# Seven block products in place of eight for the down product of both feed-forward blocks, and another order of the state space products

## What is computed

```
h = h + 0.5 * (silu(n @ w_gate) * (n @ w_up)) @ w_down     # n = RMSNorm(h), d_ff = 2816; first block
z = RMSNorm(h) @ w_in                                       # latents, u, gates
attn = attention of the latents; ssm = GLU(GELU(S5 forward(u) + S5 backward(u) + D * u))
h = h + (sig(g_a) * attn @ W_oa + sig(g_s) * ssm @ W_os) @ W_out
h = h + 0.5 * SwiGLU(RMSNorm(h))                            # second block
out = RMSNorm(h)
```

## Time and profile before

| | us |
|---|---|
| median of three runs | 2460.91 (2458.86 to 2461.21) |
| the profiled execution, its own time | 2459.75 |
| its span in the trace | 2457.8 |
| TensorE busy | 2233.3 |
| VectorE busy | 1286.4 |
| ScalarE busy | 863.3 |
| GpSimd busy | 580.9 |
| mean granted clock of TensorE, share of 2.4 GHz | 0.955 |

### The profile page before, as it was taken

How to read it: one execution, slowest core, us unless ns; L and a number is a source line. 1 busy time by engine, 2 the same in 40 slices (tenths; PEclk the granted TensorE clock), 3 DMA queues, 4 the chain that set the end, 5 groups by cost and what they waited for, 6 DMA issues and landing times. The chain is left out here.

```text
span 2457.8 us, 27322 instructions
## 1 busy us (share of the span) xinstructions
PE 2233.3 (91%) x10338; PEld 1853.9 (75%) x10338; DVE 1286.4 (52%) x1944; ACT 863.3 (35%) x1396; POOL 580.9 (24%) x500
## 2 busy tenths in 40 slices
PE   4999999989996969998958998799599999999997
PEld 3878888868885968887847776577488888878886
DVE  7675555533335226972347777451755555543444
ACT  5423232322223214143127776321432323322232
POOL 5347777600000011220002221000433233310000
PEclk8999999999997989998979999899699999999999
DMA  2323232272112363322420000241222222255111
GB/s 103 101 95 104 90 104 93 100 300 89 49 31 95 116 98 129 103 77 59 130 80 5 6 6 1 98 172 39 95 98 90 69 86 71 101 199 190 48 52 69
DMA packets 169729, 223.63 MB, mean 91 GB/s; under 512 B 32064, under 2 KB 121664, under 8 KB 169088
## 3 DMA queue, kind: packets, MB, share of 16 engines
q1 hardware_dynamic: 169600, 221.90, 27.9%
HBM read 162.58 MB, written 59.28 MB: 90 GB/s over the span
## 5 line engine op out<-in xcount | busy, mean ns | idle before, releaser
L48 PE MATMUL psum<-f_B_hi,f_A_hi 128*128 128x512 f32 x1232 | 483.7, 393 | 1.4 <-ACT rows L879 1.1
L50 PE MATMUL psum<-f_B_hi,f_A_lo 128*128 128x512 f32 x1232 | 479.8, 389 | 0.0
L49 PE MATMUL psum<-f_B_lo,f_A_hi 128*128 128x512 f32 x1232 | 479.7, 389 | 0.0
L48 PE MATMUL psum<-f_wd_hi,f_hh 128*128 128x512 f32 x704 | 275.7, 392 | 13.2 <-DVE f_hh L1030 13.2
L49 PE MATMUL psum<-f_wd_lo,f_hh 128*128 128x512 f32 x704 | 275.6, 391 | 0.0
L50 PE MATMUL psum<-f_wd_hi,f_hh 128*128 128x512 f32 x704 | 275.4, 391 | 0.0
L48 PEld LDWEIGHTS psum<-f_B_hi,f_A_hi 128*128 128x128 f32 x1232 | 231.4, 188 | 49.9 <-issue 2.5
L50 PEld LDWEIGHTS psum<-f_B_hi,f_A_lo 128*128 128x128 f32 x1232 | 231.4, 188 | 48.5
L49 PEld LDWEIGHTS psum<-f_B_lo,f_A_hi 128*128 128x128 f32 x1232 | 231.5, 188 | 47.2
L1028 DVE TENSOR_TENSOR f_wd_lo<-f_wd_raw,f_wd_hi 128x1024 fp32r<-128x1024 f32 x88 | 107.8, 1225 | 300.3 <-ACT f_wd_hi L916 300.3
L916 ACT CAST f_wd_hi<-f_wd_raw 128x1024 fp32r<-128x1024 f32 x88 | 92.8, 1054 | 360.0 <-PE psum L50 343.9
(11 more groups left out here) (306 smaller groups left out, 4079.1 us busy)
## 6 DMA issues: line engine op xcount, KB each, us to landing
f_raw<-ffn_w_gate SPq DMA_DIRECT2D x22, 1024.0 KB, 5.4
f_raw<-ffn_w_up SPq DMA_DIRECT2D x22, 1024.0 KB, 5.4
hidden<-rows SPq DMA_DIRECT2D x22, 1024.0 KB, 6.3
f_h_raw<-hidden SPq DMA_DIRECT2D x88, 256.0 KB, 2.7
f_wd_raw<-ffn_w_down SPq DMA_DIRECT2D x44, 512.0 KB, 14.3
rows<-x SPq DMA_DIRECT2D x16, 512.0 KB, 7.7
kept<-rows SPq DMA_DIRECT2D x2, 4096.0 KB, 15.3
ga_raw<-w_in SPq DMA_DIRECT2D x16, 512.0 KB, 4.3
```

The lines of the kernel that those rows point to most:

```text
L48: pe.matmul(out, lhs_hi, rhs_hi, start=first, stop=False, skip_group_check=go_on)
L49: pe.matmul(out, lhs_hi, rhs_lo, start=False, stop=False, skip_group_check=go_on)
L50: return pe.matmul(out, lhs_lo, rhs_hi, start=False, stop=last, skip_group_check=go_on)
```

## The change

- **Down product.** The 2 x 2 blocks are: token halves x column halves of the output, and inner tiles k and k + 11. Seven products q of 11 units each; unit v = 11 q + k is 4 token tiles x 3 passes = 12 matmuls of 512 columns into four banks. The weight block of products 0, 2 and 6 is a block of w_down, that of 1, 3, 4 and 5 a sum: GpSimd makes it in tt (two buffers), with one instruction in 3 and 4 and two (tu, tt) in 1 and 5; in 5 VectorE makes one more part (tv, `combine`). tt for unit v waits for the low parts of unit v - 2. Results are brought together in `evict` (from PSUM), `add_half` (rows and u1 or u2, all in SBUF) and ScalarE's `first_copy`.
- **Hidden side.** The sums of hidden blocks are made once a pair by GpSimd (`pair_sums`, four instructions of 128 x 512, between the third and the fourth weight sum of the next but one matrix), and seven blocks are stored, 1.75 MB in two transfers. Now g is stored too, and VectorE waits for the landing before product 4 of the next gate matrix.
- **Weights of gate and up.** A pair takes columns of tiles p and p + 11, so a load is two transfers with rows of 512 bytes in place of one with 1024.
- **First unit** of the down product is prepared within the last matrix, at product 4. Table steps on TensorE, ScalarE and VectorE are one slot later.
- **State space.** D table in the space of C; all 16 states first, then the wait for M and the eight products within; ScalarE's wait for u * D is gone, the load of C waits for it.

The core of the diff:

```diff
+COMBINED = (1, 3, 4, 5)
+STORED = ((0, 0), (1, 2), (0, 2), (1, 3), (1, 1), (0, 1), (0, 3))
...
-        wd = [[at("wd_hi0", [P, D], F32R, "S"), at("wd_lo0", [P, D], F32R, "S", 4 * KB)],
-              [at("wd_hi1", [P, D], F32R, "A_hi"), at("wd_lo1", [P, D], F32R, "A_lo")]]
+        wd = [[at(f"wd{u}{i}", [P, HALF], F32R, "S", 2 * KB * (2 * u + i)) for i in range(2)] for u in range(2)]
         hh = [[at(f"hh{u}{i}", [P, HALF], F32R, "ring", 2 * KB * (2 * u + i)) for i in range(2)] for u in range(2)]
-        h_raw = [at(f"h_raw{u}", [P, HALF], F32, "raw", 8 * KB * (u % 2) + 2 * KB * (u // 2)) for u in range(8)]
-        fgain, fdump = (at(n, [P, D], F32, "B_hi", 48 * KB + 4 * KB * i) for i, n in enumerate(("fgain", "fdump")))
-        UNITS = 2 * FT
+        h_raw = [at(f"h_raw{u}", [P, HALF], F32, "raw", 2 * KB * u) for u in range(8)]
+        tt = [at(f"tt{i}", [P, HALF], F32, "A_hi", 2 * KB * i) for i in range(2)]
+        tu, tv = at("tu", [P, HALF], F32, "A_hi", 4 * KB), at("tv", [P, HALF], F32, "A_hi", 6 * KB)
+        u1, u2 = at("u1", [P, QUAD, HALF], F32, "B_hi", 48 * KB), at("u2", [P, QUAD, HALF], F32, "B_lo", 48 * KB)
+        fgain, fdump = (at(n, [P, D], F32, "B_lo", 40 * KB + 4 * KB * i) for i, n in enumerate(("fgain", "fdump")))
+        left, right = slice(0, HALF), slice(HALF, D)
+        wd_block = lambda i, j, k: wd_raw[k + i * PAIRS][:, (left, right)[j]]
+        UNITS = PRODUCTS * PAIRS
...
+        unit_bank = lambda q, i: psum[:, 4 * (q % 2) + i, :]
...
             def load_matrix(n):
                 p, j = n // 2, n % 2
-                sp.dma_start(raw[j][:], weights[j][:, :, 2 * p * P:2 * (p + 1) * P]).then_inc(s_raw[j], 16)
+                for t in range(2):
+                    at = (p + t * PAIRS) * P
+                    sp.dma_start(raw[j][:, :, t * P:(t + 1) * P], weights[j][:, :, at:at + P]).then_inc(s_raw[j], 16)
+            def store_pair(p):
+                sp.wait_ge(s_hs, 4 * (p + 1))
+                sp.dma_start(hidden[p, 0].rearrange("q f s -> f q s"), h).then_inc(s_hout, 16)
+                sp.dma_start(hidden[p, 1, 1:4].rearrange("q f s -> f q s"), g[:, 1:4]).then_inc(s_hout, 16)
...
-            def load_unit(u):
-                sh, k = u // FT, u % FT
-                sp.dma_start(h_raw[u % 8][:], hidden[k // 2, QUARTER[k % 2, sh]]).then_inc(s_hraw[u % 8], 16)
-            sp.wait_ge(s_hout, 16 * (PAIRS - 1))
+            def load_unit(v):
+                q, k = v // PAIRS, v % PAIRS
+                sp.dma_start(h_raw[v % 8][:], hidden[(k,) + STORED[q]]).then_inc(s_hraw[v % 8], 16)
+            sp.wait_ge(s_hout, 32 * (PAIRS - 1))
             sp.wait_ge(s_lo, PRODUCTS * MATS)
-            for u in range(8):
-                load_unit(u)
+            for v in range(8):
+                load_unit(v)
...
+            def unit_high(v):
+                q, k = v // PAIRS, v % PAIRS
+                if v >= 2:
+                    act.wait_ge(s_unit, v - 1)
+                elif v == 0:
+                    act.wait_ge(s_lo, PRODUCTS * MATS)
+                act.wait_ge(s_hraw[v % 8], 16 * (v // 8 + 1))
+                act.copy(hh[v % 2][0][:], h_raw[v % 8][:]).then_inc(s_dhi, 1)
+                if q in COMBINED:
+                    act.wait_ge(s_tt, COMBINED.index(q) * PAIRS + k + 1)
+                    src = tt[v % 2][:]
+                else:
+                    i, j = ((0, 0), None, (1, 0), None, None, None, (1, 1))[q]
+                    t = k + i * PAIRS
+                    act.wait_ge(s_wd[t // 4], 16 * min(4, FT - t // 4 * 4))
+                    src = wd_block(i, j, k)
+                act.copy(wd[v % 2][0][:], src).then_inc(s_dhi, 1)
...
+            def unit_low(v):
+                if v >= UNITS:
+                    return
+                q, k = v // PAIRS, v % PAIRS
+                dve.wait_ge(s_dhi, 2 * v + 1)
+                dve.tensor_tensor(hh[v % 2][1][:], h_raw[v % 8][:], hh[v % 2][0][:].bitcast(F32), ALU.subtract).then_inc(s_dlo, 1)
+                i, j = ((0, 0), None, (1, 0), None, None, None, (1, 1))[q] or (0, 0)
+                dve.wait_ge(s_dhi, 2 * v + 2)
+                dve.tensor_tensor(wd[v % 2][1][:], tt[v % 2][:] if q in COMBINED else wd_block(i, j, k), wd[v % 2][0][:].bitcast(F32), ALU.subtract).then_inc(s_dlo, 1)
...
                     if q == 2 and j:
                         dve.wait_ge(s_g11, p + 1)
-                        if p:
-                            dve.wait_ge(s_hout, 16 * p)
                         dve.tensor_tensor(h[:, 0], bank(a), g[:, 0], ALU.mult).then_inc(s_h11, 1)
                     if q == 3:
                         dve.tensor_tensor(t3, bank(b), t1, ALU.add).then_inc(s_t3, 1)
                     if q == 4:
                         dve.wait_ge(s_t3, n + 1)
+                        if p and not j:
+                            dve.wait_ge(s_hout, 32 * p)
                         dve.tensor_tensor(dst[:, 1], bank(c), t3, ALU.add).then_inc(s_c22, 1)
...
+            def evict(q, i):
+
+                low_, high_ = rows[:, i, :], rows[:, QUAD + i, :]
+                tile_done(dve, q, i)
+                bank_ = unit_bank(q, i)
+                if q == 1:
+                    dve.wait_ge(s_u1, i + 1)
+                    dve.tensor_tensor(u2[:, i, :], bank_, u1[:, i, :], ALU.add).then_inc(s_u2, 1)
+                if q == 2:
+                    if i == 0:
+                        dve.wait_ge(s_res, 16 * ST)
+                    into(low_[:, left], bank_, s_o11)
+                if q == 3:
+                    dve.tensor_tensor(u1[:, i, :], bank_, u1[:, i, :], ALU.add).then_inc(s_u3, 1)
+                if q == 4:
+                    dve.wait_ge(s_half, 3 * QUAD)
+                    into(high_[:, right], bank_, s_o22)
+                if q == 5:
+                    into(high_[:, left], bank_, s_o21)
+                if q == 6:
+                    into(low_[:, right], bank_, s_o12)
+
+            def add_half(n):
+
+                i, part = n // 3, n % 3
+                if part == 0:
+                    dve.wait_ge(s_u2, i + 1)
+                    into(rows[:, i, right], u2[:, i, :], s_half)
                 else:
-                    dve.wait_ge(s_unit, (sh + 1) * FT)
-                if m == 0:
-                    dve.wait_ge(s_res, 16 * ST)
-                dve.scalar_tensor_tensor(out=two(rows[:, m, :]), in0=tile_banks(m % QUAD), scalar=0.5, in1=two(rows[:, m, :]),
-                                         op0=ALU.mult, op1=ALU.add).then_inc(s_add, 1)
-
-            def final_row(m):
-                dve.scalar_tensor_tensor(out=rows[:, m, :], in0=rows[:, m, :], scalar=stat[:, 3, m:m + 1], in1=fgain[:],
+                    dve.wait_ge(s_u3, i + 1)
+                    into(rows[:, QUAD + i, (left, right)[part - 1]], u1[:, i, :], s_half)
...
+            def combine(k):
+
+                dve.tensor_tensor(tv[:], wd_block(0, 1, k), wd_block(0, 0, k), ALU.subtract).then_inc(s_tv, 1)
+            for v in range(UNITS):
+                q, k = v // PAIRS, v % PAIRS
+                if q and k < QUAD:
+                    if q > 1:
+                        evict(q - 1, k)
+                if q == 4 and QUAD <= k < QUAD + 6:
+                    for n in (2 * (k - QUAD), 2 * (k - QUAD) + 1):
+                        add_half(n)
+                nq, nk = (v + 2) // PAIRS, (v + 2) % PAIRS
+                if nq == 5:
+                    if nk:
+                        dve.wait_ge(s_tt, COMBINED.index(5) * PAIRS + nk)
+                    combine(nk)
+                unit_low(v + 1)
...
+            def pair_sums(p):
+
+                pool.wait_ge(s_h, p + 1)
+                pool.tensor_tensor(g[:, 1], h[:, 3], h[:, 1], ALU.add).then_inc(s_hs, 1)
+                pool.tensor_tensor(g[:, 3], h[:, 0], h[:, 3], ALU.subtract).then_inc(s_hs, 1)
+                pool.wait_ge(s_hs, 4 * p + 1)
+                pool.tensor_tensor(g[:, 2], g[:, 1], h[:, 0], ALU.subtract).then_inc(s_hs, 1)
+                pool.wait_ge(s_hs, 4 * p + 3)
+                pool.tensor_tensor(h[:, 3], h[:, 2], g[:, 2], ALU.subtract).then_inc(s_hs, 1)
             for n in range(1, MATS):
-                sums(n)
+                sums(n, slice(0, 3))
+                if n >= 3 and n % 2:
+                    pair_sums((n - 3) // 2)
+                sums(n, slice(3, 4))
                 if tb and n >= 6:
                     tb.gpsimd(pool, n - 6)
+            pair_sums(PAIRS - 1)
...
+            for q in COMBINED:
+                for k in range(PAIRS):
+                    v, done = q * PAIRS + k, COMBINED.index(q) * PAIRS + k
+                    B11, B12, B21, B22 = (wd_block(i, j, k) for i in range(2) for j in range(2))
+                    if v == PAIRS:
+                        pool.wait_ge(s_mm, PRODUCTS * MATS)
+                        for group in range(len(s_wd)):
+                            pool.wait_ge(s_wd[group], 16 * min(4, FT - group * 4))
+                    if q in (1, 5) and done:
```

(56 more changed lines are left out.)

149 lines of the change are left out of this document (64 added, 85 removed).

## The result

The changed kernel takes 2509.29 us (median of 4 runs, 2506.57 to 2511.95) against 2460.13 (4 runs beside it): ratio 1.0201, 95% interval [1.0186, 1.0215]. It is slower by 49 us; 2514.0 was predicted, range 2476 to 2556. Its profiled execution has a span of 2504.8 us, 47.0 more than the earlier trace rows's 2457.8.

What follows compares the result with a forecast made beforehand. TensorE was taken to bound the kernel, busy 2233.3 of 2457.8 us. Terms -59.8 + 65 + 39 + 11 - 9 + 8 = +54 on 2459.8 gave about 2514 us, 80% range 2476 to 2556.

Steps and rivals of the forecast that it cites:

- The saving, -59.8: Both down products: 924 matmuls in place of 1056, at 0.2267 us each, save 29.9 us twice.
- The exclusion, +65: Down products 1, 4, 5: GpSimd sums and VectorE SBUF instructions exclude each other, at least 1.16 and 0.56 each; +65 (50 to 84).
- The ninth unit, +39: Unit 8 of each down product waits for its hidden tile, loaded late in SP's queue: +39 us (33 to 45).
- Hidden sums and store, +11: Gate and up: VectorE waits for the larger store after GpSimd's four sums; +8 second block, +3 first (0 to 35).
- State space, -9: State space phase: gates and scan start 9 and 12 us earlier; -9 us (-12 to -5).
- Clock, +8: Products 1 and 5: less busy TensorE sometimes gets a lower clock, as 0.74 at 78% busy; +8 us (0 to 49).
- The end, 0: After the last down matmul: smaller evictions, same squares and rows; 0, at best 1.5 us gained.
- 1 (clock): TensorE spends most of products 1 and 5 at 1.2 GHz: +41 over the forecast, 2555 us; chance 0.17.
- 2 (store 35): Gate and up: the store wait costs 35 us, not 11: 2538 us; chance 0.13.
- 3 (the ninth unit does not wait): Down products: hidden loads overtake or drain earlier, so the ninth unit does not wait: 2475 us; chance 0.06.
- 4 (no exclusion, product 1 under 3.0): Down products: GpSimd's sums never meet VectorE's instructions, product 1 units under 3.0 us: 2448 us; chance 0.08.

Runs made afterwards that it cites:

- run 1: Changed kernel with GpSimd's weight sums of products 1, 3, 4 and 5 replaced by constant fills of the same tiles: 2460.3 us, ratio 1.001.
- run 5: Changed kernel with SP issuing the ninth and tenth hidden loads before the last pair's store, units 10 to 18 after it, residual rows last: 2478.4 us, ratio 1.0081.
- run 6: Changed kernel with GpSimd's four hidden sums of each pair replaced by fills of the same tiles, waits and stores kept: 2490.9 us, ratio 1.0121.
- run 7: Changed kernel with three g blocks stored ahead of h on their own semaphore, VectorE's first g eviction waiting for that store alone: 2504.4 us.
- run 9: Changed kernel with the whole state space phase in its old order: 2524.0 us, ratio 1.0257.
- run 10: Changed kernel with final squares, variance and first four final rows two units earlier, one row to a unit: 2510.0 us.
- run 12: Changed kernel with shared sums made once, half adds spread, hidden loads before residual, g stored first, final rows earlier and table matmuls later: 2418.59 us, ratio 0.9803.

## Why the prediction was right, and where its terms were off

The sum was right to 5 us of the median with errors that cancel: the exclusion and the clock were put too high by 21, the gate and up matrices too low by 12. So the closeness of the total is in part luck. Step by step:

- **The saving, -59.8**: right. Where nothing else bounds, a unit is 12 x 0.2267 = 2.72 us; products 2, 3 and 6 have 29.9.
- **The exclusion, +65**: measured 52, 26 a block, and run 1 takes 52.6 away. Product 1 has 7.3 over its 29.9 (10 predicted), product 5 11.6 (17), product 4 7.2 (5.5; six units of 3.7 would be 5.9). The two lower bounds, 0.56 and 1.16 an instruction, were close to the measured values (0.55, 0.56 and 1.15). Product 5 was mis-sized because 4.25 was taken between the bounds of 4.0 and 4.65: its 3.99 is 3 x 0.56 + 2 x 1.16. In product 1 the unit was about right, 3.62 for 3.7 (0.18 over its lower bound, since one of GpSimd's two sums starts behind a wait and takes its full 1.29), but eight units were long and not 10.5.
- **The ninth unit, +39**: it comes 20.52 and 19.61 behind the eighth in place of 2.72, which is 34.7 more, and the matmuls at half clock behind the wait add 3.2. The prediction's own count went from the last gate or up matmul to unit 8: 53.8 and 42.9 (564.5 less 510.7, 2242.3 less 2199.4), and the trace has 52.0 and 42.6. The mechanism was right in every link, and run 5 takes it away whole. The larger store, in two pieces, cost nothing at the load behind it: 20.0 us from store to load issue against 20.5 before, and 10.8 from issue to landing, where 11.2 + 1.9 had been put.
- **Hidden sums and store, +11**: this step failed in the first block. It put +3 there ("only the two before them are late") and the trace has +19.7. The prediction asked what the sums do to the store and never what they do to VectorE, though it had the exclusion priced two paragraphs earlier: it applied it to 512-column subtractions only. About 12 are the sums passing ahead of VectorE's small table instructions of 32 and 64 columns, 4 the store, and 3.6 stay open (runs 6 and 7). A wait doesn't shrink with the instruction that waits: 0.2 us of work took 1.2. In the second block the store wait is as described but smaller, 0.36 a matrix for 0.6 to 1.
- **State space, -9**: -10.4, and run 9 gives 11.0. The scan starts 14.5 us earlier in the phase (42.2 behind its first instruction on TensorE, 56.8 before), for 12 predicted.
- **Clock, +8**: nothing in products 1 and 5, where the prediction had put it. At 79% busy in product 5 the granted clock stayed 1.00. The row with 0.74 did not carry over to a stretch with idle gaps of 0.6 to 1.0 us, one in each unit. Half clock came behind the wait of 16.6 us, and, which the prediction had not asked for, in the first block's gate and up part: 0.53 from 153 to 156, behind the wait of 5.08, and 0.63 from 198 to 201, behind one of 1.90 at L515. That is part of the +19.7.
- **The end, 0**: +3.8, VectorE's order in units half as long (run 10).

**The rivals.** 1 (clock): refuted by the windows, 1.00 in products 1 and 5. 2 (store 35): refuted, the store is 4 in each block (run 7). 3 (the ninth unit does not wait): refuted at its own sign, 16.59 us ended by the hidden tile. 4 (no exclusion, product 1 under 3.0): refuted, 3.62.

Still open: why the executions fall into two patterns of matrices 2, 4 and 6 in the first block, what makes the 3.6 us that run 6 leaves there, and where the 7 us of run 12 come from. None was tried.

## What to carry to other kernels

A unit cut in half halves the cover of everything that hid behind it. Before such a cut, list for each engine what stands in one unit, and price each meeting of a GpSimd instruction that reads SBUF with a VectorE instruction by the length of the GpSimd one, the small instructions above all. Then look at SP's queue: a load that had a whole long unit of time may now be the first thing that is late, and moving it can cost nothing (run 5). Last, share sums across units before spreading them: here 66 sums to 44 was worth 35 us, and only after that did spreading the half adds pay.

## What the runs showed of the hardware

- A GpSimd instruction that only writes SBUF did not hold VectorE up at all, at equal length (three fills, 1.69 us, across three VectorE instructions, each at its own duration). One that reads it did, whole but for about 0.14 us: a subtraction of 0.69 ended 0.55 after the sum that it had met.
- VectorE's copy of 64 x 64, with one SBUF input, was held up by a GpSimd sum like the instructions with two (1.01 for 0.19); with the sums as fills (run 6) all such copies take 0.19. The prediction had counted two-input instructions only.
- The granted clock stayed 1.00 through 41 us with TensorE busy 79% and an idle gap of 0.94 to 0.98 us in every unit. Behind waits of 5.08 and 1.90 us, in the first block's gate and up part, it was 0.53 and 0.63 over 3 us.
